# The S5 mixer of a decoder trunk in 256 chunks of four tokens instead of 128 chunks of eight

## The reference

```python
dt = jnp.exp(log_dt)[:, None]
mag, ang = jnp.exp(ar * dt), ai * dt
abr, abi = mag * jnp.cos(ang), mag * jnp.sin(ang)          # step of the state, per group and state
...
xr = jnp.einsum('blgp,gnp->blgn', uf, bbr)                 # inputs of the states
xi = jnp.einsum('blgp,gnp->blgn', uf, bbi)
_, _, hr, hi = lax.associative_scan(combine, (a_r, a_i, xr, xi), axis=1)   # h[t] = a h[t-1] + x[t]
y = (jnp.einsum('blgn,gpn->blgp', hr, c_re) - jnp.einsum('blgn,gpn->blgp', hi, c_im) + d_skip * uf)
y = jax.nn.gelu(y.reshape(bsz, seq, S5_WIDTH))
y = y * jax.nn.sigmoid(y @ glu_w + glu_b)
```

## Time and profile before

| | us |
|---|---|
| median of three runs | 2715.64 |
| lowest and highest of them | 2711.79, 2717.36 |
| the profiled execution, its own time | 2709.55 |
| span of its profile | 2707.8 |
| TensorE busy | 2575.2 |
| VectorE busy | 1551.7 |
| GpSimd busy | 1312.4 |
| ScalarE busy | 1019.2 |

### The profile page before, as it was taken

The page is one execution under the profiler, slowest core; times in us unless marked ns, Lnnn a source line. Parts: engine busy times, 40 slices in busy tenths (PEclk is TensorE's granted clock), DMA queues, the critical chain, the costliest instruction groups (busy, mean ns, idle before and its releaser), DMA issues. The chain is left out here.

```text
span 2707.8 us, 34637 instructions
## 1 busy us (share of the span) xinstructions
PE 2575.2 (95%) x13515; PEld 2025.7 (75%) x13515; DVE 1551.7 (57%) x2691; ACT 1019.2 (38%) x1478; POOL 1312.4 (48%) x818
## 2 busy tenths in 40 slices
PE   8899889989999999999999999998999999999998
PEld 6667656767777777777777887766777777888887
DVE  4768777789997225844331394668899922211112
ACT  5232354233444533324344422432434354322222
POOL 3332244454454464535555532543546446655654
PEclk9989999999999999999999999999999999999999
DMA  5242113122222163323222342222222215333332
GB/s 163 72 133 58 40 57 92 51 75 65 76 76 71 51 191 87 86 63 95 85 82 82 86 129 56 81 60 63 78 65 76 71 51 184 89 97 102 101 117 86
DMA packets 385666, 232.92 MB, mean 86 GB/s; under 512 B 29592, under 2 KB 371552, under 8 KB 383072
## 3 DMA queue, kind: packets, MB, share of 16 engines
q1 hardware_dynamic: 385136, 229.62, 28.7%
q10 hardware_dynamic: 368, 1.08, 0.1%
HBM read 213.88 MB, written 14.69 MB: 84 GB/s over the span
## 5 line engine op out<-in xcount | busy, mean ns | idle before, releaser
L709 POOL TENSOR_TENSOR w_lo<-w_raw,w_hi 128x1024 fp32r<-128x1024 f32 (+2 forms) x408 | 902.2, 2212 | 1244.1 <-ACT w_hi L820 1244.1
L1744 PE MATMUL psum<-h_hi,w_hi 128*128 128x512 f32 x1984 | 799.3, 403 | 18.1 <-DVE scratch L1250 7.9
L820 ACT ACTIVATE w_hi<-w_raw 128x1024 fp32r<-128x1024 f32 (+2 forms) x408 | 397.3, 974 | 1092.7 <-PE psum L1744 1050.6
L1744 PE MATMUL psum<-h_lo,w_hi 128*128 128x512 f32 x1984 | 767.0, 393 | 0.9 <-POOL h_lo L717 0.9
L1744 PE MATMUL psum<-h_hi,w_lo 128*128 128x512 f32 x1984 | 515.1, 390 | 0.0
L1744 PEld LDWEIGHTS psum<-h_hi,w_hi 128*128 128x128 f32 x1984 | 377.0, 190 | 130.7 <-issue 35.4
L1744 PEld LDWEIGHTS psum<-h_lo,w_hi 128*128 128x128 f32 x1984 | 375.9, 190 | 79.3 <-issue 2.0
L1744 PEld LDWEIGHTS psum<-h_hi,w_lo 128*128 128x128 f32 x1984 | 373.9, 188 | 76.7
L1344 DVE MAX8 top<-scores 128x8 f32<-128x512 f32 (+5 forms) x352 | 324.0, 920 | 6.7
L1346 DVE MATCH_REPLACE8 scores<-top,scores 128x512 f32<-128x512 f32 (+5 forms) x352 | 318.8, 906 | 0.0
L1744 PE MATMUL psum<-a_hi,w_hi 128*128 128x512 f32 x704 | 286.5, 407 | 18.4 <-ACT w_hi L820 8.3
(11 more groups left out here) (310 smaller groups left out, 2946.7 us busy)
## 6 DMA issues: line engine op xcount, KB each, us to landing
w_raw<-in_w_ffn_in_dram SPq DMA_DIRECT2D x176, 512.0 KB, 3.8
w_raw<-in_w_ffn_out_dram SPq DMA_DIRECT2D x96, 384.0 KB, 3.1
w_raw<-in_w_in_dram SPq DMA_DIRECT2D x68, 512.0 KB, 3.8
w_raw<-in_w_out_dram SPq DMA_DIRECT2D x32, 512.0 KB, 3.6
x_half<-xs SPq DMA_DIRECT2D x8, 1024.0 KB, 7.0
xs<-x_half SPq DMA_DIRECT2D x8, 1024.0 KB, 6.5
w_raw<-in_w_ffn_out_dram SPq DMA_DIRECT2D x32, 256.0 KB, 2.6
out_dram<-mixed SPq DMA_DIRECT2D x8, 512.0 KB, 3.6
```

The source lines that it names most:

```text
L709: eng.tensor_tensor(w_lo(u, n), w_raw[:, u % 3, 0:n], w_hi[:, u % 2, 0:n].bitcast(F32), ALU.subtract).then_inc(sems["weights_ready"], 1)
L820: act(w_hi[:, u % 2, 0:n], w_raw[:, u % 3, 0:n], ACTF.Copy).then_inc(sems["hi_ready"], 1)
L1744: return eng.matmul(out_, lhsT, rhs, start=start, stop=stop, skip_group_check=True)
```

## The change

A chunk has four tokens and there are 256 of them. The powers go to 4 (three complex products instead of seven). The rotation doubles once more, to 256 columns; the last doubling is made in two pieces of 64 columns a state group. Z, Vt and Kt have half their size: eight turned matrices a half instead of sixteen, eight tap products, convolution over lags 0 to 3, and one pass of `outputs` where there were two. Products of r = 2 and r = 6 are 32 with 256 columns. Ht, Gt and Et have twice their size, so the operations of r = 4 and r = 5 come twice, for two state groups each (`pairs`), and the eight scans run over 256 chunks. The states' inputs use the four banks C0, C1, D0, D1, each half of whose 512 columns is one part (real, imaginary). The temporaries `Xt` move from `scratch` to `scores`, and the `prep_tmp` of the preparation goes. PLAN is unchanged.

The diff, cut to its core (reshapes with the literal 8 become `S5_STEPS` throughout; the last pieces are TensorE's):

```diff
-S5_STEPS = 8
+
+S5_STEPS = 4
+S5_CHUNKS = T // S5_STEPS
...
-        Z = part(area, 0, (2, 8, 4, 32), "p (c m q e) -> p c m q e", c=2, m=8, q=4)
+        Z = part(area, 0, (2, S5_STEPS, 4, 32), "p (c m q e) -> p c m q e", c=2, m=S5_STEPS, q=4)
         Z2 = part(area, 0, (2, T), "p (m t) -> p m t", m=2)
-        Vt = part(area, 2048, (8, 2, P), "p (m c s) -> p m c s", m=8, c=2)
-        Gt = part(area, 2048, (2, 4, P), "p (c q s) -> p c q s", c=2, q=4)
-        Kt = part(area, 4096, (8, P), "p (m s) -> p m s", m=8)
-        Et = part(area, 5120, (2, 4, P), "p (c q s) -> p c q s", c=2, q=4)
-        prep_tmp = part(area, 4096, (2, 512), "p (a c) -> p a c", a=2)
+        Kt = part(area, 1024, (S5_STEPS, P), "p (m s) -> p m s", m=S5_STEPS)
+        Vt = part(area, 2048, (S5_STEPS, 2, P), "p (m c s) -> p m c s", m=S5_STEPS, c=2)
+        Gt = part(area, 2048, (2, 4, S5_CHUNKS), "p (c q s) -> p c q s", c=2, q=4)
+        Et = part(area, 4096, (2, 4, S5_CHUNKS), "p (c q s) -> p c q s", c=2, q=4)
...
-        Ht = part(scratch, 4096, (2, 4, P), "p (c q s) -> p c q s", c=2, q=4)
-        Xt = part(scratch, 5120, (2, 512), "p (a c) -> p a c", a=2)
+        Ht = part(scratch, 4096, (2, 4, S5_CHUNKS), "p (c q s) -> p c q s", c=2, q=4)
...
+        Xt = part(scores_, 2304, (2, 512), "p (a c) -> p a c", a=2)
...
-                        act(Vt[:, :, c, :], bank(g).rearrange("p (m s) -> p m s", m=8), ACTF.Copy).then_inc(
+                        act(Vt[:, :, c, :], bank(g, 0, 512).rearrange("p (m s) -> p m s", m=S5_STEPS), ACTF.Copy).then_inc(
...
-                        o = 512 * (q % 2)
-                        act(Ht[:, :, q, :], bank("CD"[q // 2], o, o + 256).rearrange("p (c s) -> p c s", c=2),
+                        act(Ht[:, :, q, :], bank(S5_BANKS[q]).rearrange("p (c s) -> p c s", c=2),
...
-                    for k, n in ((2, 2), (4, 4)):
-                        for j in range(n):
-                            cmul(sp[PR + k + 1 + j], sp[PI + k + 1 + j], sp[PR + 1 + j], sp[PI + 1 + j],
-                                 sp[PR + k], sp[PI + k], t1, t2, t3, t4)
+                    for j in range(2):
+                        cmul(sp[PR + 3 + j], sp[PI + 3 + j], sp[PR + 1 + j], sp[PI + 1 + j],
+                             sp[PR + 2], sp[PI + 2], t1, t2, t3, t4)
...
-                    for k in range(6):
+                    for k in range(7):
...
-            def rotations(hh, first, last, place):
+            def rotations(hh, first, last):
 
                 qs = slice(4 * hh, 4 * hh + 4)
                 for k in range(first, last):
                     n = 1 << k
-                    sh = [P, 4, n]
+                    w = min(n, 64)
+                    sh = [P, 4, w]
                     rr, ri = (s5p[:, o + k, qs].unsqueeze(2).broadcast_to(sh) for o in (RR, RI))
-                    t_ = [place[:, i // 2, (i % 2) * 256:(i % 2) * 256 + 4 * n].rearrange("p (q c) -> p q c", q=4)
+                    t_ = [Xt[:, i // 2, (i % 2) * 256:(i % 2) * 256 + 4 * w].rearrange("p (q c) -> p q c", q=4)
                           for i in range(4)]
-                    cmul(Et[:, 0, :, n:2 * n], Et[:, 1, :, n:2 * n], Et[:, 0, :, 0:n], Et[:, 1, :, 0:n],
-                         rr, ri, *t_)
-
-            def inputs(g, c, place):
-
-                za, zb = (place[:, i, :].rearrange("p (m q e) -> p m q e", m=8, q=4) for i in range(2))
+                    for a in range(0, n, w):
+                        b = a + n
+                        cmul(Et[:, 0, :, b:b + w], Et[:, 1, :, b:b + w], Et[:, 0, :, a:a + w], Et[:, 1, :, a:a + w],
+                             rr, ri, *t_)
...
-                    rotations(0, 0, 5, prep_tmp)
+                    rotations(0, 0, 6)
                 elif n == 3:
-                    rotations(0, 5, 7, prep_tmp)
+                    rotations(0, 6, 8)
...
-                def outputs(m):
-                    ya, yb = (t.rearrange("p (m q e) -> p m q e", m=4, q=4) for t in (fa, fb))
-                    sl = slice(1 + 4 * m, 5 + 4 * m)
+                def outputs():
...
-                    rotations(hh, 0, 5, Xt)
+                    rotations(hh, 0, 6)
...
-                    outputs(0)
-                if r == 3:
-                    outputs(1)
-                    if hh:
-                        rotations(hh, 5, 7, Xt)
+                    outputs()
+                if r == 3 and hh:
+                    rotations(hh, 6, 8)
...
-                    tt(fa, er, hr, MUL)
-                    link(tt(fb, ei, hi, MUL))
-                    link(tt(gr, fa, fb, ADD))
-                    tt(fa, er, hi, MUL)
-                    link(tt(fb, ei, hr, MUL))
-                    link(tt(gi, fa, fb, SUB))
+                    for rows_ in pairs:
+                        (er, ei), (hr, hi), (gr, gi) = ((flat(t, 0, rows_), flat(t, 1, rows_)) for t in (Et, Ht, Gt))
+                        tt(fa, er, hr, MUL)
+                        link(tt(fb, ei, hi, MUL))
+                        link(tt(gr, fa, fb, ADD))
+                        tt(fa, er, hi, MUL)
+                        link(tt(fb, ei, hr, MUL))
+                        link(tt(gi, fa, fb, SUB))
...
-                            decay = mag8[:, 4 * hh + q:4 * hh + q + 1].broadcast_to([P, P])
+                            decay = mag_chunk[:, 4 * hh + q:4 * hh + q + 1].broadcast_to([P, S5_CHUNKS])
...
-                    tt(fa, er, hr, MUL)
-                    link(tt(fb, ei, hi, MUL))
-                    x4 = [t.rearrange("p (q c) -> p q c", q=4)[:, :, 0:P - 1] for t in (fa, fb)]
+                    last = S5_CHUNKS - 1
                     eng.memset(Gt[:, 0, :, 0:1], 0.0)
                     eng.memset(Gt[:, 1, :, 0:1], 0.0)
-                    link(tt(Gt[:, 0, :, 1:P], x4[0], x4[1], SUB))
-                    tt(fa, er, hi, MUL)
-                    link(tt(fb, ei, hr, MUL))
-                    tt(Gt[:, 1, :, 1:P], x4[0], x4[1], ADD).then_inc(sems["hprev_ready"], 1)
+                    x2 = [t.rearrange("p (q c) -> p q c", q=2)[:, :, 0:last] for t in (fa, fb)]
+                    for rows_ in pairs:
+                        (er, ei), (hr, hi) = ((flat(t, 0, rows_), flat(t, 1, rows_)) for t in (Et, Ht))
+                        tt(fa, er, hr, MUL)
+                        link(tt(fb, ei, hi, MUL))
+                        link(tt(Gt[:, 0, rows_, 1:], x2[0], x2[1], SUB))
+                        tt(fa, er, hi, MUL)
+                        link(tt(fb, ei, hr, MUL))
+                        ins = tt(Gt[:, 1, rows_, 1:], x2[0], x2[1], ADD)
+                        if rows_ is pairs[0]:
+                            link(ins)
+                    ins.then_inc(sems["hprev_ready"], 1)
...
-                        for m in range(8):
+                        for m in range(S5_STEPS):
...
-                        for j in range(8):
+                        for j in range(S5_STEPS):
                             for q in range(4):
                                 rows_ = slice(32 * q, 32 * q + 32)
-                                o = 512 * (q % 2) + c * P
-                                ins = mm(bank("CD"[q // 2], o, o + P), Vt[rows_, 7 - j, c, :], u_[rows_, j, :],
-                                         j == 0, j == 7)
+                                ins = mm(bank(S5_BANKS[q], c * S5_CHUNKS, (c + 1) * S5_CHUNKS),
+                                         Vt[rows_, S5_STEPS - 1 - j, c, :], u_[rows_, j, :], j == 0, j == S5_STEPS - 1)
...
-                    for lag in range(8):
-                        for j0, j1 in ((lag, 4), (max(lag, 4), 8)):
+                    half = S5_STEPS // 2
+                    for lag in range(S5_STEPS):
+                        for j0, j1 in ((lag, half), (max(lag, half), S5_STEPS)):
                             if j0 < j1:
-                                mm(bank("C", j0 * P, j1 * P), Kt[:, lag, :], u_[:, j0 - lag:j1 - lag, :], lag == 0, False)
+                                mm(bank("C", j0 * S5_CHUNKS, j1 * S5_CHUNKS), Kt[:, lag, :], u_[:, j0 - lag:j1 - lag, :], lag == 0, False)
...
-                    for j in range(8):
-                        o = bank("C", j * P, (j + 1) * P)
+                    for j in range(S5_STEPS):
+                        o = bank("C", j * S5_CHUNKS, (j + 1) * S5_CHUNKS)
```

More of the change, by code:

```diff
@@ L1620, in outputs @@
                     link(tt(yb, power(1, sl, ys), ni_, MUL))
-                    flat = [Z[hh][:, c, 4 * m:4 * m + 4, :, :].rearrange("p m q e -> p (m q e)") for c in range(2)]
+                    flat = [Z[hh][:, c, :, :, :].rearrange("p m q e -> p (m q e)") for c in range(2)]
                     link(tt(flat[0], fa, fb, ADD))
```

53 lines of the change are left out of this document (28 added, 25 removed).

## The result

| | before | after |
|---|---|---|
| median, us | 2713.72 (four runs) | 2753.12 (four runs, 2751.22 to 2754.69) |
| ratio of the medians, 95% interval | | 1.0147 [1.0133, 1.0160] |
| profiled execution, span | 2709.55, 2707.8 | 2754.69, 2752.6 |

What follows compares the result with a forecast made beforehand. It took VectorE, last at three of four meetings with TensorE, to set the time in the S5 stretches. Terms -2.8 + 14.1 + 1.7 + 5.5 + 0.9 = +19.4 us took the median from 2715.64 to 2735.0, range 2720 to 2747.

Steps and rivals of the forecast that it cites:

- the meetings: Four places, one per channel half and layer, where TensorE's step 6 products wait for VectorE's shifted states of step 5.
- TensorE's pieces: Savings in each half: convolution 3.5 us, tap products 1.9, transposes 0.95; together 6.35, or 25.4 in all.
- the chain of layer 0's second half: VectorE from mask product to shifted states: +8.7 us of work, +2.1 for a stretched record.
- the shared port: VectorE products held by GpSimd's weight remainder: one more stretch of 2.1 us at each of four chain ends, bounds 0 and 4.3.
- All of it is gained: -2.8: Layer 0: four fewer complex products for the step's powers, ahead of a 7.95 us TensorE wait, save 2.8 us.
- about even: Layer 0, between the halves: TensorE starts 5.8 us late but is 3.2 us faster up to the second half's mask product.
- the mask product is 3.5 us late: Layer 0, second half: VectorE arrives 7.8 us late, 4.2 us of idle time covers most, leaving 3.5.
- clock term: Layer 0: after TensorE's long wait its products run at the lower clock level, +1.7 us on the path.
- 5.5 + 0.9: Layer 1: second half's shifted states come 5.5 us after TensorE needs them, plus 0.9 us for the lower clock, partly hidden.
- Part of this TensorE waits already at bank B: Layer 1, first half: part of the +6.9 us falls at bank B, which VectorE empties in order behind step 4.
- TensorE's busy time down by over 20 us: Sign named for the forecast: TensorE's busy time over the kernel falls by more than 20 us.
- Rival 3: Each chain meets two remainders more, TensorE restarts at half clock after each wait: 2751 us, chance 0.05.

Runs made afterwards that it cites:

- e1: Kernel after, with GpSimd making only 16 of 1024 weight-remainder columns in the second token half's projections (work left out): 2698.0 us, 0.9946 of before.
- e14: Kernel after, with GpSimd filling the 1024 raw columns with zeros instead of making the remainder in the second token half's projections (work left out): 2695.1 us.
- e15: Kernel after, with GpSimd copying the weights' high part instead of making the remainder in the second token half's projections (work left out): 2717.0 us.
- e6: Kernel after, layer 1's steps from r = 4 of the first half one projection unit later, from r = 6 of the second half two: 2757.2 us.
- e9: Kernel after, with twelve selection rounds for block 3 moved from between layer 0's S5 steps to ahead of them: 2744.3 us.

## Why the prediction was half of the result

**Right.** That TensorE's gains are not collected, since VectorE is last at the meetings; TensorE's pieces; the scans (4.7 us forecast, 4.76 in e1); the chain of layer 0's second half, 28.7 + 8.7 + 2.1 = 39.5 forecast, 40.0 measured (one remainder more, 2.6 us for the 2.1); the wait of over 10 us ahead of its state products (14.2).

**Wrong: the shared port, "+2.1 at each of the four ends".** The step took one more meeting for each chain, 8.4 us in all. Chain by chain they were +8.3, +2.6, 0 and +7.0 us, 17.9 in all. In the first chain the kernel before had met four remainders, three of them in part only (5.4 us), and the kernel after met seven (13.7 us). e1, e14 and e15 make this the cause: with meetings at no cost the loss is not merely smaller, it is nil. And each chain hands its delay on, at more than its own price.

**Wrong: layer 0, "All of it is gained: -2.8".** The wait at 125 us fell even by 4.7, but by 213 us this was lost again. ScalarE, kernel after:

```profile
210.36 0.22 ACT L1075 ACTIVATE gsum<-gsum 128x16 f32<-128x16 f32 x1 [9.64 <-DVE gsum L1463]
```

ScalarE waits there for a retention step that stands behind the late rotations on VectorE, and behind it in its own queue stand the copies of the turned matrices, for which TensorE waited 7.2 us instead of the 3.0 of the earlier trace rows. The rotations were costed in VectorE's chain alone, not for who is queued behind those who wait for VectorE.

**Wrong: layer 0's hand-over, "about even", "the mask product is 3.5 us late".** With the first shifted states 13.1 us later (250.00 to 263.14) and their products at the half clock, which was counted for the second half alone, TensorE's own path carried the delay: taps at 276.36, mask product 8.3 us late where 0.7 would have stood by the sum (3.5 - 2.8). (The sum also handed on VectorE's 7.9 us without the 2.1 that it had just added; TensorE came last there, so this changed nothing.) From there on the forecast holds (+11.3 for 10.8), and with a clock term of 2.2 for 1.7 the mark A is 21.7 instead of 13.0 late.

**Wrong: layer 1, 5.5 + 0.9.** Measured 16.4 + 2.4. The mask product of the second half was 9.5 us late for 3.7, since the prediction had no wait of TensorE for the first mask product (4.8) with the half clock behind it, and "Part of this TensorE waits already at bank B" was 9.4 us. The chain then grew by 15.9 for 10.8, the meetings again. The place of one of these, that at 1603 us, makes up some 5 of the 12 us by itself.

**Wrong: "TensorE's busy time down by over 20 us".** It fell by 13.5. TensorE's pieces are shorter as forecast, but the products behind the waits took longer at the half clock: 2.5, 2.2 and 2.4 us in three groups of state products, 2.5 in the inputs of the states at 1608 us.

Rival 3 had these mechanisms, two remainders more in each chain and the half clock behind each wait, and gave 2751; it had a chance of 0.05. It gave every chain the same share, and the shares were not the same. What stays open: 1.7 us between A and B and 2.7 behind C in the profiled pair, whose distance of 44.8 us is also larger than the 39.4 of the medians. In the twenty profiles the part from A to B lasts between 1237.8 and 1244.3 us and the part behind C between 1006.7 and 1015.8, without order in the edits, so no cause can be read from one pair.

## What to carry to other kernels

Before work is moved to VectorE as products with two inputs in SBUF, count GpSimd's two-input instructions in those stretches and take each that can meet one as met, at its whole length: in the kernel after VectorE met each of the seven that started from 198 to 263 us, in full or in part, and each of the three from mask product to shifted states in the second half. Put one input of such a product into PSUM where a bank is free, and follow a delay over every engine's queue to the next meeting, with the half clock behind each new long wait. Moving other work away from a chain helps only as far as that work stood in the chain.

## What the hardware showed that was not expected

- The scan with two SBUF inputs is held by GpSimd as a product is (one of eight took 2.76 us for 0.67), its form with data in PSUM is not. It takes 0.66 us for 256 and 0.40 for 128 elements, about 2.05 ns for each more.
- GpSimd's fill of 1024 columns (0.95 us) holds nothing, its copy (1.04 us alone) holds VectorE for some 0.8 us.
- Which of two products a remainder holds, the one ahead of the mask or one behind it, turned on less than 0.1 us of phase and was worth 3 to 5 us in layer 1. In the same place it fell one way in three profiles (after, e6, e9) and the other way in seven.
